# Hybrid decoder trunk: the first eight column units of the input projection streamed as row units, each beside its adaLN unit

## The reference

```python
cond = silu(c)                                    # c: (1, 1024)
mod = cond @ ada_w[l] + ada_b[l]                  # adaLN: six vectors of 1024
sh_m, sc_m, g_m, sh_f, sc_f, g_f = split(mod, 6)
h = rms_norm(x, mix_pre_g[l]) * (1 + sc_m) + sh_m
z = h @ w_in[l]                                   # 1024 x (30 * 256 + 16) columns
...                                               # conv, stick-breaking attention, gated linear
                                                  # attention, gates, three branches, w_o
x = x + g_m * rms_norm(y, mix_post_g[l])
h = rms_norm(x, ffn_pre_g[l]) * (1 + sc_f) + sh_f
y = swiglu(h) if l == 0 else moe_swiglu(h)        # dense FFN, then 8 experts
x = x + g_f * rms_norm(y, ffn_post_g[l])
```

## Time and profile before

| what | us |
|---|---|
| median of three runs | 1874.24 (1873.97 to 1874.91) |
| the profiled execution | 1875.42, its span 1873.7 |
| PE busy | 1790.7 |
| DVE busy | 1552.3 |
| ACT busy | 1131.6 |
| POOL busy | 190.7 |
| first matmul of the projection | 40.19 |

### The profile page before, as it was taken

One profiled execution on the slowest core, in us unless ns is written; L12 is line 12 of the kernel. 1 busy time (PEld: TensorE's weight loads), 2 busy tenths in 40 slices (PEclk: granted clock), 3 DMA queues, 4 the chain that ended last, 5 costly groups with the idle time before them and its releaser, 6 DMA issues.

```text
span 1873.7 us, 28698 instructions
## 1 busy us (share of the span) xinstructions
PE 1790.7 (96%) x10848; PEld 1586.8 (85%) x10849; DVE 1552.3 (83%) x1442; ACT 1131.6 (60%) x951; POOL 190.7 (10%) x156
## 2 busy tenths in 40 slices
PE   2999998899989999988999999999999999999997
PEld 2999998899979999977888888888888888888885
DVE  6998876999557667777888888898898988988986
ACT  3444564433354545655777777777777677777774
POOL 0395001000005900010000000000000000000000
PEclk8999999899999999998999999999999999999999
DMA  9965534699625434443999989989989899898992
GB/s 377 358 239 192 179 136 157 230 382 365 239 93 188 146 132 139 145 148 112 362 370 345 378 337 362 379 323 377 371 330 378 327 369 376 336 373 344 361 373 86
DMA packets 72523, 525.30 MB, mean 280 GB/s; under 512 B 8113, under 2 KB 8241, under 8 KB 8705
## 3 DMA queue, kind: packets, MB, share of 16 engines
q1 hardware_dynamic: 72288, 524.03, 73.8%
q0 software_dynamic: 160, 0.23, 0.0%
HBM read 523.17 MB, written 1.05 MB: 280 GB/s over the span
## 4 chain that ended last, share of the span: by engine, by line
PE 55%; DVE 2%; ACT 0%; issue 0%; DVEq 0%; ACTq 0%
PE bank L1634 33%; PE bank L1649 16%; PE bank L1669 2%; PE bank L1659 1%; PE bank L1371 1%; PE bank L1342 1%; PE bank L1689 0%; PE bank L1690 0%; PE bank L1605 0%; DVE arena L935 0%; DVE arena L912 0%; DVE arena L939 0%; DVE arena L1058 0%; DVE w_lo L869 0%; DVE arena L1050 0%
## 5 line engine op out<-in xcount | busy, mean ns | idle before, releaser
L1119 DVE TENSOR_TENSOR w_lo<-raw,w_hi 128x2048 fp32r<-128x2048 f32 x224 | 510.1, 2291 | 86.4 <-ACT w_hi L744 86.3
L744 ACT ACTIVATE w_hi<-raw 128x2048 fp32r<-128x2048 f32 x224 | 428.6, 1917 | 98.9 <-PE bank L1649 70.4
L1371 PE MATMUL bank<-acts,w_hi 128*128 128x256 f32 x2080 | 375.8, 285 | 35.4 <-DVE acts L925 26.4
L1371 PEld LDWEIGHTS bank<-acts,w_hi 128*128 128x128 f32 x2080 | 323.9, 193 | 40.6 <-issue 29.9
L1634 PE MATMUL bank<-acts 128*128 128x512 f32 x1248 | 304.3, 393 | 0.0
L1634 PE MATMUL bank<-w_hi,acts 128*128 128x512 f32 x960 | 297.2, 391 | 1.5 <-DVE acts L1263 1.5
L1371 PE MATMUL bank<-acts,w_lo 128*128 128x256 f32 x1040 | 293.8, 283 | 0.0
L1119 DVE TENSOR_TENSOR acts<-raw,acts 128x2048 fp32r<-128x2048 f32 x112 | 256.2, 2287 | 20.3 <-ACT acts L744 20.3
L1634 PEld LDWEIGHTS bank<-acts 128*128 128x128 f32 x1248 | 231.3, 188 | 46.7
L744 ACT ACTIVATE acts<-raw 128x2048 fp32r<-128x2048 f32 x112 | 215.1, 1920 | 72.4 <-PE bank L1634 69.9
L1649 PE MATMUL bank<-w_hi,acts 128*128 128x512 f32 x832 | 256.1, 389 | 0.0
(11 more groups left out here) (237 smaller groups left out, 2149.7 us busy)
## 6 DMA issues: line engine op xcount, KB each, us to landing
raw<-in_experts SPq DMA_DIRECT2D x336, 1024.0 KB, 5.0
raw<-in_stream SPq DMA_DIRECT2D x161, 1024.0 KB, 5.8
arena<-in_x_t SPq DMA_DIRECT2D x1, 1024.0 KB, 11.8
out_t<-arena SPq DMA_DIRECT2D x2, 512.0 KB, 2.6
arena<-in_c_row SPq DMA_DIRECT2D x1, 512.0 KB, 4.6
arena<-in_vecs SPq DMA_DIRECT2D x1, 224.0 KB, 2.5
arena<-in_glr_w POOLq DMA_DIRECT2D x2, 64.0 KB, 4.2
arena<-in_a POOLq DMA_DIRECT2D x2, 32.0 KB, 4.4
```

The lines of the kernel that those rows point to most:

```text
L744: act.activation(expert_hi[s], raw[:, slot, :], ACT.Copy).then_inc(hi_written, 1)
L1119: dve.tensor_tensor(expert_lo[s], raw[:, slot, :], f32(expert_hi[s]), ALU.subtract).then_inc(raw_taken, 1)
L1371: mm = pe.matmul(out[:, c, :], w[:, 256 * k + P * c:256 * k + P * c + P], (hi if high else lo)[:, k, :], start=(k == 0 and n == 0 and c == 0),
```

## The change

For layer 0 the first 2048 columns of `w_in` (column units 0 to 7) are laid out by rows: unit `("zk", 0, k, 0)` holds row chunk k of all 2048 columns. The stream opens with adaLN unit 0, row unit 0, adaLN unit 1, row unit 1 and so on. After each adaLN unit of group 0, DVE finishes bias and gain for that chunk alone, scales that chunk of x, and ACT shifts it; PE multiplies row unit k by chunk k and adds to sixteen half banks, that is to all eight banks. x is loaded first, in two halves, and the Silu of c stands behind the first norm. Five matmuls of constants stand ahead of the norm's sums. The low-rank product moves behind column unit 8, and DVE's and POOL's taps start after it (DVE's at unit 9). The two GLU sigmoids have a buffer each. Of groups 1 and 2, twelve units ride behind column units 9 to 20; group 2 is cut so that its first four give the FFN's scale, and the last four (the FFN's gate) move into the dense FFN.

```diff
-    units = [("ada", 0, 0, k) for k in range(KC)]
+    units = []
+    for k in range(KC):
+        units += [("ada", 0, 0, k), ("zk", 0, k, 0)]
...
+        later = [("ada", 0, 1, k) for k in range(KC)] + [("ada", 0, 2, k) for k in range(4)]
+        for u in range(FIRST if layer == 0 else 0, Z_UNITS + G_UNITS):
             units.append(("z", layer, u, 0))
-            if later and (u < 9 or u % 2):
+            if layer == 0 and u > FIRST and later:
                 units.append(later.pop(0))
...
-            later = [("ada", 1, g, k) for g in range(3) for k in range(KC)]
+            later = [("ada", 0, 2, k) for k in range(4, KC)]
+            later += [("ada", 1, g, k) for g in range(3) for k in range(KC)]
...
-            act.wait_ge(vec_loaded, 16)
+            act.wait_ge(consts, 5)
+            norm_x(0)
             act.wait_ge(cond_loaded, 16)
             act.activation(cond[0], cond[0], ACT.Silu).then_inc(cond_ready, 1)
-            act.wait_ge(consts, 5)
-            act.wait_ge(x_loaded, 16)
-            norm_x(0)
+            act.wait_ge(vec_loaded, 16)
+            for k in range(KC):
+                shift_chunk(0, SH_M, 1, k)
+                write_hi(("zk", 0, k, 0))
             for layer in range(DEPTH):
                 units = mixer_units(layer)
-                for i in range(len(units)):
+                if layer == 0:
+                    hook(layer, 1)
+                    write_hi(units[FIRST])
+                    for i in (0, 2, 4, 5, 6, 7):
+                        evacuate(layer, i, units[i])
+                        if i == 2:
+                            hook(layer, 6)
...
+            def finish_mixer_in(layer, k):
...
+                dve.wait_ge(raw_taken, POS["ada", layer, 0, k] + 1)
...
+                link(dve.tensor_tensor(pair, pair, bias, ALU.add))
+                link(dve.scalar_tensor_tensor(mod(layer, A_M)[:, k:k + 1], mod(layer, SC_M)[:, k:k + 1], 1.0,
+                                              vec(layer, "mix_pre_g")[:, k:k + 1], ALU.add, ALU.mult))
...
-                        first = (4, 4, 6)[c]
+                        first = (4, 4, 6)[c] if layer else FIRST + 1
...
+            dve.wait_ge(vec_loaded, 16)
+            for k in range(KC):
+                add_ada(next(order))
+                if k == 0:
+                    reciprocal_rms()
+                finish_mixer_in(0, k)
+                scale_chunk(0, A_M, k)
+                take(("zk", 0, k, 0))
+                split_chunk(1, k)
...
+            def project_rows(k):
+
+                u = ("zk", 0, k, 0)
+                pe.wait_ge(raw_taken, POS[u] + 1)
+                pe.wait_ge(h_split, k + 1)
+                s = SLOT[u]
+                for c in range(2 * FIRST):
+                    out = two(bank[c // 2])[:, c % 2, :]
+                    for n, (w, high) in enumerate(parts(s)):
+                        mm = pe.matmul(out, w[:, P * c:P * c + P], (h_hi if high else h_lo)[:, k, :],
+                                       start=(k == 0 and n == 0 and c % 2 == 0),
+                                       stop=(k == KC - 1 and n == 2), skip_group_check=True)
+                    if k == KC - 1 and c % 2 and c < 2 * FIRST - 1:
+                        mm.then_inc(columns_done, 1)
+                mm.then_inc(consumed, 1)
...
+            for _ in range(5):
+                pe.matmul(bank[0][:, :], ones, area(C_ID, 4 * P), start=True, stop=True)
             norm_sums()
+            pe.wait_ge(norm_root, 1)
+            for k in range(KC):
+                project_rows(k)
```

More of the change, by code:

```diff
@@ L60 @@
 PAIRS = D_FF // 256
+FIRST = 8
 O_SB = 2 * CONV
@@ L100, in plan, with ada_groups @@
     return units
+def ada_groups(g, k):
+    if g == 2:
+        return [16 * g + 8 * (k // 4) + 2 * (k % 4) + j for j in range(2)]
+    return [16 * g + 8 * j + k for j in range(2)]
 PLAN = plan()
+ADA_IN_FFN = [("ada", 0, 2, k) for k in range(4, KC)]
 N_UNITS = len(PLAN)
@@ L239, in program @@
         conv_acc, conv_tmp = area(A_H, 4, T), area(A_H + 1024, 4, T)
-        sig = area(A_ST, 2, T)
+        sig = [area(A_ST + 512 * i, 2, T) for i in range(2)]
         stick_e = [area(A_ST + 512 * i, 2, T) for i in range(2)]
@@ L369, in mixer_units @@
         def mixer_units(layer):
-            return [u for u in W_UNITS if u[1] == layer and u[0] in ("z", "out", "wo")]
+            first = [("z", 0, u, 0) for u in range(FIRST if layer == 0 else 0)]
+            return first + [u for u in W_UNITS if u[1] == layer and u[0] in ("z", "out", "wo")]
         def mixer_place(u):
             return mixer_units(u[1]).index(u)
-        BANKS = {}
-        used = [0] * 7
+        BANKS = {("z", 0, u, 0): [(u, 0)] for u in range(FIRST)}
+        used = [1] * 8
         turn_of = 0
-        for u in W_UNITS:
+        for u in W_UNITS[FIRST:]:
             if u[0] == "out" and mixer_place(u) % 3 != 1:
@@ L563, in shift, with shift_chunk @@
                 for c in range(KC):
[L564 to L568, removed]
+                    shift_chunk(layer, b, count, c, split_too)
+            def shift_chunk(layer, b, count, c, split_too=True):
+                act.wait_ge(h_scaled, KC * (count - 1) + c + 1)
+                bias = mod(layer, b)[:, c:c + 1]
+                if split_too:
+                    act.activation(h_hi[:, c, :], hf[:, c, :], ACT.Identity, bias=bias)
+                act.activation(hf[:, c, :], hf[:, c, :], ACT.Identity, bias=bias).then_inc(h_ready, 1)
             def merged_high(layer, half):
@@ L585, in evacuate @@
                 if u[0] == "z" and i in (0, 2):
-                    if i == 2:
-                        wait_read(act, ("z", layer, 1, 0))
-                    copy_unit(u, sig, ACT.Sigmoid)
+                    copy_unit(u, sig[i // 2], ACT.Sigmoid)
                 elif u[0] == "z" and 4 <= i < 10:
@@ L764, in _ @@
                         hook(layer, i)
+                    if layer == 0 and i == FIRST + 1:
+                        hook(layer, 2)
                 if layer == 0:
@@ L1538, in hook @@
                     if i == 10:
-                        wait_read(pe, ("z", layer, 7, 0))
+                        for j in (3, 4, 5, 6, 7):
+                            wait_read(pe, ("z", layer, j, 0))
                     if i == 12:
@@ L1566, in _ @@
                 for i, u in enumerate(mixer_units(layer)):
+                    if layer == 0 and i < FIRST:
+                        continue
                     if i == 0:
```

154 lines of the change are left out of this document (93 added, 61 removed).

## The result

| | before | after |
|---|---|---|
| median of five runs, us | 1874.24 | 1887.67 |
| lowest to highest | 1873.97 to 1875.10 | 1883.31 to 1891.55 |
| profiled execution (span) | 1875.42 (1873.7) | 1887.67 (1885.8) |

The ratio is 1.0068, 95% interval 1.005 to 1.0086: slower by 13.4 us in the medians and 12.3 us in the profiled executions. Run again word for word, the changed kernel gave a median of 1883.61 beside 1874.29 (1.0052, 1.0039 to 1.0066), so the size lies between 9 and 13 us. The forecast was 8.3 us, to 1882.5. Measured against its ranges, 1887.67 lies just above the own range (1878 to 1887) and inside the whole one (1874 to 1889), and 1883.61 lies inside both.

The account below looks back on a forecast made before the run. The prediction took PE and DVE as nearly equal queues in the mixer's projection, with DVE binding after the change: the state update 8.3 us later, 0 behind it, 1883.7 profiled, 1882.5 us median. Own range 1878 to 1887, whole range 1874 to 1889.

Parts of the forecast that it names:

- own range: 1878 to 1887 us, from start (-2.2, +2), period (7 x -0.2, +0.4), clock (-0.9, +0.9) and contact of the queues (-1, +3).
- Step 1: At the start: the norm's sums end near 12.0 and DVE's first adaLN unit starts at 14.9 us, against 9.67 before.
- Step 2: Row-unit chunk loop: ACT and DVE take turns, 8.63 us per chunk; the eighth chunk ends at 85.6.
- Step 3: PE behind the chunk loop: last rows end at 92.4, unit 8 and the low-rank product at 101.9 us.
- Rival 3: In the row chunks the clock stays low, so PE binds: rows end near 111, 18.6 us more, 1901; chance 5%.
- Step 4: DVE's queue to the state update: 85.6 + 143.6 + 1.1 + 5.4 = 235.7 against 227.4, 8.3 us later.
- Step 5: Behind the milestone, DVE's state update: the delay is carried whole, with 0 us of added cost.
- The FFN term: Four adaLN units moved into the dense FFN cost 0 there; uncovered they would cost 9.2 us.
- rival 1: In the mixer PE's path alone binds: milestone 0.8 to 2.5 us later, about 1876, no measurable change; chance 16%.
- rival 2: In the chunk loop ACT and DVE overlap: period 5.84 us, 11.2 us faster, 1863; chance 8%.
- rival 4: In the FFN DVE's idle time is unusable for the moved adaLN units: up to 9.2 us more, 1892; chance 4%.

Follow-up runs that it names:

- Experiment 1: Changed kernel with ACT writing the high half of row unit k+1 right behind the shifts of chunk k; median 1862.56 us, ratio 0.9943 to the kernel before.
- experiment 3: Changed kernel without 30 of the 31 taps of one of DVE's three channel groups in the first layer; median 1876.53 us.
- experiment 5: Changed kernel with the four adaLN units moved back from the dense FFN into the mixer, behind units 21 to 24; median 1897.84 us, ratio 1.0118.
- experiment 11: Changed kernel with 30 of 31 of GpSimd's first-layer taps cut to two columns each; median 1876.66 us.
- experiment 10: Changed kernel with two matmuls of constants in PE's gap before DVE's state update; median 1883.29 us, profiled 1887.83.
- experiment 9: Kernel of experiment 7 with two matmuls of constants in the gap ahead of the milestone; median 1859.56 us, ratio 0.9921 to the kernel before.
- experiment 7: Changed kernel with high halves one chunk ahead and the Silu of c ahead of the norm's root; median 1862.68 us.
- experiment 2: Changed kernel with the Silu of c ahead of the norm's root; median 1884.26 us, profiled 1884.37.
- experiment 6: Kernel before with the regrouping alone: group 2 cut anew, its four last adaLN units moved into the dense FFN; median 1873.80 us, ratio 0.9997.
- experiment 8: Kernel of experiment 7 with unit 9's high half ahead of the copies of units 4 to 7; median 1859.31 us.
- third edit: Unit 9's high half written ahead of the copies of units 4 to 7, added to the kernel of experiment 7; median 1859.31 us.

## Why the prediction was right, and where it was off

**Direction and mechanism were right.** The forecast was that ACT and DVE would take turns, that this would put the last rows near 92, and that DVE's in-order queue would carry the delay past PE's path. Experiment 1 took the turns away, and DVE's waits with them, and the milestone came 23.3 us sooner; experiments 3, 5 and 11 made DVE's queue shorter and longer and the milestone followed, until at 227.4 to 228.6 PE's path counted again, directly or through ACT's logarithm.

**Step 1** (start at 14.9): 15.51. ACT began to square x at 5.27, well ahead of the 7.8 that I had for its load, and it gained nothing: PE's constants and sums held the root back to 12.64, where I had 12.0. **Step 2** (period 8.63): 8.61; DVE idles 2.78 of it, as put. The last chunk's split starts at 85.80, so DVE goes on at 86.14 (85.6). **Step 3**: rows end at 93.45 (92.4). I counted half of the clock's cost behind the last gap, 0.85 us; in the profiled execution it was 1.4, the last 48 matmuls taking 7.09 us where 5.7 is the full clock's. The clock stayed out of the period, as put: the first chunk took PE 8.2 us and the others 5.7 to 7.4, inside 8.61. Rival 3 did not come, but four of the eight chunks ran in part at the lower clock, and the first of them left PE only 0.45 us idle.

**Step 4**: 235.7 against 238.24 measured. Of the 2.5 us too little, 0.5 are the start and the period, 1.5 are busy time and 0.5 idle time. Busy time was 145.07 against 143.6. I took seven low halves and four adaLN units out at undisturbed lengths, but those that stayed ran longer than before: a low half 2432 and 2489 ns in the mean for 2367, an adaLN half 1366 for 1319. More of the queue now lies beside GpSimd's taps, and experiment 11 shows that these stretch it. Idle time was 7.0 against 6.5. The seam took 6.2 where I had 5.4, since DVE also waited 0.9 us before each GLU product; the short gaps took 0.9. My 1.1 for them was a slip as well, since 11.6 less 7.4 and 2.7 leaves 1.5. This step was the larger part of what was off.

**Step 5** had 0 behind the milestone; in the profiled execution it was 1.2 us (10.9 at the milestone, 12.1 at the end). PE waits longer for the state update, 2.13 us for 0.86, and the clock fell in the block behind: 6.11 us for 4.49. That is 1.6 us. Later stretches gave some of it back, 0.6 between the mixer's last norm and the first down product (50.33 us for 50.90). Together with the 2.5 us up to the milestone this is all but some 0.2 of the 4.0 us by which the profiled execution passed its forecast of 1883.7. But it is a sum of stretches and not a shown cause: experiment 10 took the block's 1.6 us away and the end did not move. In experiment 5 the block cost 4.1 us (8.55). In the kernel with the high halves and the Silu ahead, filling the gap took it away and 2.65 us of it reached the end (experiment 9). The FFN term, 0, was right (experiment 5).

**The median** was 5.2 us above the forecast in the first five runs and 1.1 above in the second. Its ten executions reach over 8.5 us, from 1883.01 to 1891.55; the kernel before reached over 3.5, 3.0 and 5.1 us in its three lots of fifteen. In the kernels with the high halves ahead experiments 7 and 9 point to the clock behind the milestone's gap. For the changed kernel they don't carry over, since filling the gap left 1883.0 to 1887.8 and the times don't go with the mean clock. That stays open: its traced executions took 1887.67, 1887.67 and, with the gap filled, 1887.83, and none near 1883.5 was traced. So the 1.1 us between the forecast and the second median say little about its terms. The traced execution of that lot was 4.0 above.

**The range.** Added up straight, the four terms of my own range reach from 1877 to 1891; I wrote 1878 to 1887, and 1887.67 was measured.

**The rivals.** 1 failed because DVE's queue is the longer (experiment 3). 2 was excluded by order of code and became true when the order was changed: at a period of 5.74 the milestone came 23.3 us sooner where I had 19.5, because the first chunk's wait went too. That 1862.56 stands beside the 1863 worked out is partly luck: the start of the sum was 1 to 5 us too low, and the gain 21 to 25 us where I had 19.5. 3 did not come (above), and 4 fell with experiment 5, in which the FFN is no shorter without the four units.

## What to carry to other kernels

Interleaving the two streams paid here only when an engine's part of chunk k+1 could be done before the other engine needed it: 8.61 us a chunk with the engines taking turns, 5.74 without. So write out both in-order queues and add up the loop before counting what the third engine gains. An operand that needs no input from the loop (here a weight's high half) belongs one turn ahead. Behind the loop two engines were nearly full for 140 us, and what the one with the longer queue lost or won ahead of that stretch was carried whole to its end (experiments 1 and 2). What was saved where the other engine's path was the longer was waited away again (experiments 6 and 8). The two quickest versions have the high halves and the Silu ahead, one with the third edit (median 1859.3 us) and one with PE's gap filled (1859.6), both 0.8% under the kernel before. The second has the smaller spread, 1.7 us for 6.1.

## What the runs showed of the hardware that was not expected

GpSimd made DVE's instructions longer, not only now and then: 90 taps took 49.0 us beside its full-width taps and 37.9 with those cut to two columns (experiment 11), an adaLN half 1366 ns and 1218, six taps in a row 3.37 us and 2.46. The softplus, which reads one operand from PSUM, was not slowed (544 ns in the mean beside the full taps, 558 beside the cut ones). The Trainium skill says this of the memory ("SBUF — State Buffer", section "Who interferes with whom"): a DVE instruction with two inputs in SBUF contends with a GpSimd instruction that reads SBUF, one with a single SBUF input outside the two-port modes doesn't. Both halves agree with these rows.

The clock's cost stood behind the gap, in what came next, and the gap's length alone didn't set it. The same forty matmuls behind PE's wait for the state update took:

| kernel | gap, us | granted clock | block, us |
|---|---|---|---|
| before | 0.86 | 1.00 | 4.49 |
| changed, gap filled (10) | 0.41 | 1.00 | 4.49 |
| GpSimd's taps cut (11) | 2.13 | 1.00 | 4.49 |
| changed | 2.13 | 0.72 | 6.11 |
| high halves and Silu ahead (7) | 2.12 | 0.50 | 8.64 |
| four units back (5) | 4.84 | 0.50 | 8.55 |
